# Where the operands of a split-float32 block kernel start in on-chip memory: multiples of 512 bytes

## The chip, the cores and the metric

One Trainium2 chip, one of its cores. The kernel is a hand-scheduled program for the five engines of that core: TensorE (PE, with its weight loads as PEld), VectorE (DVE), ScalarE (ACT), GpSimd (POOL) and SyncE (SP, used here to issue transfers). The metric is the device time of one execution in microseconds; times of the same kernel are medians of several runs.

## What is computed

The reference runs two transformer-like blocks over 256 tokens of 1024 features in float32.

```python
def reference(x, ...):
    x = first_block(x, ...)    # RMSNorm, gated delta rule (4 heads) and causal pooling, w_out;
                               # RMSNorm, product-key experts: 16,384 experts, 8 heads, top 16 of 128 x 128 keys;
                               # RMSNorm
    return second_block(x, ...)  # RMSNorm, block attention (8 heads) and retention (4 heads), w_out;
                                 # RMSNorm, FFN of 2816 with a depthwise convolution and GELU;
                                 # per-layer embedding with a sigmoid gate; RMSNorm
```

The experts in the reference are gathered per token; their core is

```python
u = expert_down[idx]
v = expert_up[idx]
act = jax.nn.gelu(jnp.einsum("td,thkd->thk", xb, u).astype(jnp.float32), approximate=False)
return jnp.einsum("thk,thkd->td", (gate * act).astype(v.dtype), v)
```

## The kernel before, in words

**Weights as a stream of tiles.** All weights are laid out as 412 tiles of 128 x 1024 float32, in the order of use: 20 tiles of the first projection, 8 of the first output projection, 16 of the query, 128 of `expert_down`, 128 of `expert_up`, then the second block (8 + 8 + 12 tiles of its input projections, 8 of its output projection, 1 of the embedding, 22 triples of up, gate and down, 1 of the embedding, 8 of its gate). The experts are not gathered: every expert is computed for every token, and a dense table of gates, zero but for the chosen ones, multiplies the result.

**Splitting.** A float32 product is made of three products of the type `fp32r`. SP loads a tile into one of four slots of `raw` (L335). ACT rounds it into `whi` (L443), and DVE subtracts, giving `wlo` (L456); each has four slots. The activations are split in the same way into `ahi` and `alo`, each expert's row of `ea` into `phi` (ACT, L1289) and `plo` (DVE, L1854), and the embedding's operand into `pthi` and `ptlo` once. The helper `products` (L459 to L462) issues the three matmuls:

```python
nc.tensor.matmul(out_ap, wh, xh, start=first, stop=False, skip_group_check=True)
nc.tensor.matmul(out_ap, wh, xl, start=False, stop=False, skip_group_check=True)
return nc.tensor.matmul(out_ap, wl, xh, start=False, stop=last, skip_group_check=True)
```

The second argument is the stationary operand, the third the moving one. There are two uses. `gemm_tile` makes 24 products per weight tile: stationary 128 columns of `whi` or `wlo`, moving 256 columns of `ahi` or `alo`. `token_rows` makes 12 per weight tile: stationary 128 tokens of an activation, moving 512 columns of `whi` or `wlo`. The activation is `ahi`/`alo` in the output projections, the values and the embedding's gate, `phi`/`plo` in the 128 tiles of `expert_up` and the 22 down tiles of the FFN, and `pthi`/`ptlo` in the 2 embedding tiles (these call `products` at L1018). A small product at the start has the 8 columns of `gw_hi` or `gw_lo` stationary and `ahi` or `alo` moving. All other products are plain float32.

**Addresses.** `place` gives every buffer the same start in each of the 128 partitions. It rounds sizes up to 32 bytes and puts the next buffer behind. The first free byte is 16,481, rounded up to 16,512. By these sizes `raw`, `whi`, `wlo`, `ahi`, `alo`, `ident` and `ones` all start 128 bytes past a multiple of 512, as does every 128-column slice of them. `vec` (772 bytes, rounded to 800), `warm` and `wm` (32 each) come next, so `xt`, `pf`, `phi`, `plo` and the arena `ea` start 480 past a multiple of 512. The arena is reused by the stages; there `pthi` and `ptlo` start 96 past, `AmT2` 32 past, `gbc` 448 past, and the slices of `gw_hi` and `gw_lo`, 32 bytes each, at various multiples of 32.

**Order of the work.** Each engine has its own program, in order; semaphores join them. ACT may refill `whi` slot j once PE has finished the tile four before (`w_used`); SP refills `raw` once both halves of the split are made. A 16-way scatter per head puts the gates into the dense table in DRAM: POOL issues 256 indirect transfers (L409), 128 for each half of the tokens. POOL does some of the second half's between heads of the first, the rest after. SP fetches gates for four experts at a time into `gd` (L343); for tiles 0 to 87 of `expert_up` those of the first half of the tokens, since the rows of the second half need the second chain of scatters. Ahead of the pair of fetches of tile 88 SP waits for that chain:

```python
with sp.Fori(1, SPLIT // 8) as j:
    up_pair(j, P)
sp.wait_ge(s["scat1"], 16 * TOPK * NH)
with sp.Fori(SPLIT // 8, N_EXP // 8) as j:
    up_pair(j, T)
```

`up_pair` issues both the fetches of gates and the loads of the weight tiles, so a wait there holds back the weights as well. DVE multiplies `ea` by `gd` (L1850), ACT makes `phi`, DVE `plo`, PE the 12 products.

`ones` is filled by DVE at the start (L1496). PE uses it for idle products at the start (L577) and for sums over partitions in the first block's mixer (L631, L740). ACT reads one element of it in six short activations (L1118 and others) that have the engine's tables loaded ahead of time.

Of the kernel before, what the change touches and what calls it, by code (L numbers as in the profile page):

```python
# [20 lines left out]
ACT = mybir.ActivationFunctionType  # L21
AX = mybir.AxisListType

P = 128
# [3 lines left out]
KT = D // P  # L28
# [54 lines left out]
N_CV = _c  # L83
# [16 lines left out]
def program(nc, x_tok, vecs, wts, c1, gate_w, rows, w_pool, keys, c2, ple_t, nrows, out):  # L100
    ctx = ExitStack()
    with ctx:
        s = {n: ctx.enter_context(nc.semaphore("s_" + n)) for n in SEMS}


        top = [-(-nc.sbuf_base // 32) * 32]
        slab = ctx.enter_context(nc.sbuf_tensor("slab", [P, (nc.sbuf_bytes_remaining - 64) // 4], F32))

        def place(name, shape, dt=F32, at=None):
            size = int(np.prod(shape)) * (2 if dt == F16 else 4)  # L110
            size = -(-size // 32) * 32
            if at is None:
                at, top[0] = top[0], top[0] + size
            else:
                at[0], at = at[0] + size, at[0]
            return nc.alloc_sbuf_tensor_at(name, [P] + list(shape), dt, offset=at)

        raw = place("raw", [2, 2 * TW])
        whi = place("whi", [RING, TW], F32R)
        wlo = place("wlo", [RING, TW], F32R)  # L120
        ahi = place("ahi", [KT, T], F32R)
        alo = place("alo", [KT, T], F32R)
        ident = place("ident", [P])
        ones = place("ones", [P])
        vec = place("vec", [N_CV])
        warm = place("warm", [8])
        wm = place("wm", [KT])
        eps = warm[:, 6:7]
        small = top[0]
        xt = place("xt", [TB, D])  # L130
        pf = place("pf", [2, T])
# [35 lines left out]
        arena = top[0]  # L167
        ea = place("ea", [N_EXP, T])
        end = top[0]
        assert end <= nc.sbuf_usable_end, end  # L170

        a = [arena]
        h32 = place("h32", [KT, T], at=a)
# [50 lines left out]
        gw_lo = place("gw_lo", [KT, 8], F32R, at=a)  # L224
        ba = place("ba", [T], at=a)
        tok = place("tok", [160], at=a)
        assert a[0] <= end, a[0] - end
        col = {}
        c = 0
# [7 lines left out]
        a = [common]  # L237
# [4 lines left out]
        a = [arena + 4 * T * sc_at]  # L242
# [3 lines left out]
        a = [common]  # L246
# [57 lines left out]
        def half_row(buf, b0):  # L304

            return buf[:, b0 // 2, (b0 % 2) * 512:(b0 % 2 + 1) * 512]
# [799 lines left out]
        def _(act):  # L1106
            A = nc.scalar.activation

            def row_squares(i, c, src, junk):

                A(junk, src, ACT.Square, accum_out=ss[:, i, c:c + 1]).then_inc(s["t_sq"], 1)
# [3 lines left out]
                A(root[:, i, tb:tb + 1], ss[:, i, c:c + 1], ACT.Sqrt, scale=1.0 / D, bias=bias).then_inc(s["t_root"], 1)  # L1115

            act.wait_ge(s["ones_ready"], 1)
            A(warm[:, 0:1], ones[:, 0:1], ACT.Sqrt)  # L1118
            act.wait_ge(s["x_in"], 16)
            row_squares(0, 0, xt[:, 0, :], sq_t[:, 0, :])  # L1120
            act.wait_ge(s["t_sq"], 1)
# [15 lines left out]
            def hi_for(u):  # L1137

                split_hi(act, u + LEAD, (u + LEAD) % 4)
# [62 lines left out]
            def pool_rows(p):  # L1202

                act.wait_ge(s["pool_ps"], p + 1)
                for g in (2 * p, 2 * p + 1):
                    m = A(h32[:, DH + g, :], bank(0, T, base=g * T), ACT.Copy, scale=vcol("pool_scale", g))
                m.then_inc(s["mix_pool"], 1)
                act.wait_ge(s["mix_pool"], p + 1)
                operand_act(act, 1, h32, QUARTERS[p])

            pool_rows(0)
            A(warm[:, 7:8], ones[:, 0:1], ACT.Sqrt)
            for p in range(2):
                act.wait_ge(s["o_ps"], 2 * p + 2)
                A(sq[:, 2 * p:2 * p + 2, :], bank(6 + p, 2 * T).rearrange("p (h t) -> p h t", h=2), ACT.Square)\
# [117 lines left out]
                turned_act(act, 3, q, mid_weight)  # L1333
            hi_for(W_V2 - 1)
            hi_for(W_V2)
            A(warm[:, 2:3], ones[:, 0:1], ACT.Sqrt)
            for tb in range(TB):
                act.wait_ge(s["xd"], 3 + tb)
                row_squares(2, tb, xt[:, tb, :], sq_t[:, tb, :])
# [111 lines left out]
            for q in range(2, 4):  # L1451
                turned_act(act, 6, q, ple_weight)
            hi_for(W_PLEG)
            A(warm[:, 3:4], ones[:, 0:1], ACT.Sqrt)
            for tb in range(TB):
                act.wait_ge((s["xa"], s["xd"])[tb], (2, 6)[tb])
                row_squares(6, tb, xt[:, tb, :], sq_t[:, tb, :])
# [1 line left out]
            A(root[:, 6, :], ss[:, 6, 0:TB], ACT.Sqrt, scale=1.0 / D, bias=eps).then_inc(s["t_root"], 1)  # L1459
            for n in range(1, KT):  # L1460
                hi_for(W_PLEG + n)
            A(warm[:, 4:5], ones[:, 0:1], ACT.Sigmoid)
            act.wait_ge(s["t_r"], 9)
            for b0 in range(3):
                act.wait_ge(s["gate_ps"], b0 + 1)
# [4 lines left out]
            for c in range(2):  # L1470
# [3 lines left out]
                if c == 0:  # L1474
                    act.wait_ge(s["x5"], 3)
                    row_squares(7, 2, half_row(xt, 2), half_row(sq_t, 2))
            A(warm[:, 5:6], ones[:, 0:1], ACT.Sqrt)  # L1477
            act.wait_ge(s["t_sq"], 16)
            act.wait_ge(s["t_pre"], 4)
            row_root(7, 0, 1, pre[:, 3, 0:1])  # L1480
# [708 lines left out]
```

## Time and profile before

| | us |
|---|---|
| median of 3 runs | 1329.18 |
| lowest, highest | 1328.83, 1330.32 |
| profiled execution: span from first to last instruction | 1327.4 |
| TensorE matmul busy | 1310.4 |
| VectorE busy | 943.1 |
| ScalarE busy | 725.3 |
| GpSimd busy | 517.7 |

The median counts the whole execution, the span only what lies between the first and the last instruction of one profiled execution; this one's own time outside the span is not given beside it. Busy time of TensorE is the union of its matmuls, whose ends are modelled: a duration of one matmul is longer than the distance to the next one's start. The granted clock of TensorE is written in tenths of full speed. Line numbers (L456) are those of the kernel before.

### The profile page before, as it was taken

The numbers are of one execution on the slowest core, as the hardware profiler recorded it, in microseconds if no ns is written. First come the engines' busy times: TensorE is split into PE (matmuls) and PEld (weight loads), VectorE is DVE, ScalarE is ACT, GpSimd is POOL, SyncE is SP. The second block draws the span as 40 slices with busy tenths as digits, with TensorE's granted clock in tenths as the row PEclk, the third lists the DMA queues.
The fourth block names the chain that finished last, engine by engine and source line by source line (L and its number), as shares of the span: only waits on it lengthen the run. The fifth ranks groups of instructions, "written<-read, shape, count | busy, mean of one in ns | idle before, by whom it ended". The sixth has DMA issues, their size and how long they took to land. (4 is left out here: it accounts for less than half of the span.)

```text
span 1327.4 us, 26387 instructions
## 1 busy us (share of the span) xinstructions
PE 1310.4 (99%) x8853; PEld 1196.9 (90%) x8853; DVE 943.1 (71%) x1766; ACT 725.3 (55%) x1077; POOL 517.7 (39%) x276
## 2 busy tenths in 40 slices
PE   8999999999999999999999999999999999999997
PEld 8999899999999999998888888788789888999986
DVE  6885677999998467766666666666666667676665
ACT  6833557777777743344444444444465446444446
POOL 1010002888887888787787778100000000000000
PEclk9999999999999999999999999999999999999999
DMA  7459554777767766668777778777674335555551
GB/s 257 149 194 383 197 175 154 180 185 184 183 177 186 191 168 153 142 146 216 209 208 211 213 213 209 262 234 228 213 242 162 112 115 183 181 188 183 184 191 64
DMA packets 119325, 253.03 MB, mean 191 GB/s; under 512 B 44336, under 2 KB 60848, under 8 KB 118752
## 3 DMA queue, kind: packets, MB, share of 16 engines
q1 hardware_dynamic: 77232, 229.24, 53.5%
q0 software_dynamic: 42032, 22.99, 10.9%
q8 instruction: 36, 0.59, 0.2%
q14 instruction: 25, 0.20, 0.0%
HBM read 234.23 MB, written 17.96 MB: 190 GB/s over the span
## 5 line engine op out<-in xcount | busy, mean ns | idle before, releaser
L456 DVE TENSOR_TENSOR wlo<-raw,whi 128x1024 fp32r<-128x1024 f32 x412 | 503.1, 1223 | 156.3 <-ACT whi L443 147.5
L443 ACT ACTIVATE whi<-raw 128x1024 fp32r<-128x1024 f32 x412 | 435.1, 1058 | 305.8 <-PE ps L462 292.8
L409 POOL DMA_INDIRECT gates_dense<-gate,spot x256 | 506.1, 1977 | 170.2 <-issue 78.7
L460 PE MATMUL ps<-ahi,whi 128*128 128x256 f32 x1824 | 522.5, 286 | 2.9 <-DVE alo L537 2.6
L461 PE MATMUL ps<-alo,whi 128*128 128x256 f32 x1824 | 515.9, 283 | 0.0
L462 PE MATMUL ps<-ahi,wlo 128*128 128x256 f32 x1824 | 515.7, 283 | 0.0
L460 PEld LDWEIGHTS ps<-ahi,whi 128*128 128x128 f32 x1824 | 349.9, 192 | 7.5 <-issue 5.8
L461 PEld LDWEIGHTS ps<-alo,whi 128*128 128x128 f32 x1824 | 349.4, 192 | 0.9
L462 PEld LDWEIGHTS ps<-ahi,wlo 128*128 128x128 f32 x1824 | 349.4, 192 | 0.0
L460 PE MATMUL ps<-whi,phi 128*128 128x512 f32 x600 | 238.2, 397 | 1.2 <-DVE plo L1854 1.1
L462 PE MATMUL ps<-whi,plo 128*128 128x512 f32 x600 | 237.8, 396 | 0.0
L461 PE MATMUL ps<-wlo,phi 128*128 128x512 f32 x600 | 237.7, 396 | 0.0
L1854 DVE TENSOR_TENSOR plo<-ea,phi 128x256 fp32r<-128x256 f32 x128 | 54.5, 426 | 126.9 <-ACT phi L1289 120.2
L460 PEld LDWEIGHTS ps<-whi,phi 128*128 128x128 f32 x600 | 113.0, 188 | 28.8 <-issue 1.1
L462 PEld LDWEIGHTS ps<-whi,plo 128*128 128x128 f32 x600 | 113.0, 188 | 27.5
L461 PEld LDWEIGHTS ps<-wlo,phi 128*128 128x128 f32 x600 | 113.1, 188 | 26.5
L1278 ACT ACTIVATE ea<-ps 128x256 f32 x120 | 46.1, 384 | 134.5 <-PE ps L462 134.3
L460 PE MATMUL ps<-whi,ahi 128*128 128x512 f32 (+1 forms) x136 | 52.4, 385 | 0.1
L461 PE MATMUL ps<-wlo,ahi 128*128 128x512 f32 (+1 forms) x136 | 51.3, 377 | 0.0
L462 PE MATMUL ps<-whi,alo 128*128 128x512 f32 (+1 forms) x136 | 51.3, 377 | 0.0
L427 POOL DMA_DIRECT2D wrow<-in_nrows x1 | 0.6, 580 | 126.6 <-DVE plo L1854 126.6
L1289 ACT ACTIVATE phi<-ea 128x256 fp32r x120 | 47.9, 399 | 0.0
(367 smaller groups left out, 1088.0 us busy)
## 6 DMA issues: line engine op xcount, KB each, us to landing
raw<-in_wts SPq DMA_DIRECT2D x412, 512.0 KB, 3.7
gates_dense<-pf POOLq DMA_DIRECT2D x4, 4096.0 KB, 30.8
gd<-gates_dense SPq DMA_DIRECT2D x22, 256.0 KB, 4.8
gd<-gates_dense SPq DMA_DIRECT2D x10, 512.0 KB, 5.8
gates_dense<-gate,spot POOLq DMA_INDIRECT x256
cst<-in_c POOLq DMA_DIRECT2D x1, 1216.0 KB, 6.5
xt<-in_x_tok SPq DMA_DIRECT2D x2, 512.0 KB, 4.5
kk<-in_keys POOLq DMA_DIRECT2D x1, 1024.0 KB, 5.2
```

The lines of the kernel that those rows point to most:

```text
L409: pl.indirect_dma_start(out=dense, out_offset=bass.IndirectOffsetOnAxis(ap=spot[:, tb, h, k:k + 1], axis=0), in_=gate[:, tb, h, k:k + 1], ...
L427: pl.dma_start(wrow[:, :, :].rearrange("p a n -> p (a n)"), nrows.partition_broadcast(P)).then_inc(s["nrows_in"], 16)
L443: nc.scalar.activation(whi[:, j, :], raw_tile(j // 2, j % 2), ACT.Copy).then_inc(s["w_hi"], 1)
L456: nc.vector.tensor_tensor(wlo[:, j, :], raw_tile(j // 2, j % 2), whi[:, j, :].bitcast(F32), ALU.subtract).then_inc(s["w_lo"], 1)
L460: nc.tensor.matmul(out_ap, wh, xh, start=first, stop=False, skip_group_check=True)
L461: nc.tensor.matmul(out_ap, wh, xl, start=False, stop=False, skip_group_check=True)
L462: return nc.tensor.matmul(out_ap, wl, xh, start=False, stop=last, skip_group_check=True)
L1278: A(row_of(quad * 4 + n), late(n if four else n % 2, T), ACT.Gelu).then_inc(s["gelu"], 1)
L1289: A(phi[:, n % 2, :], row_of(quad * 4 + n), ACT.Copy).then_inc(s["p_hi"], 1)
L1854: V.tensor_tensor(plo[:, n % 2, :], row_of(oct_ * 8 + n), phi[:, n % 2, :].bitcast(F32), ALU.subtract)\
```

## The change

`place` rounds the start of every buffer of 1024 bytes or more up to a multiple of 512, in the main area and in the arena. The small buffers `vec`, `warm` and `wm` move ahead of the weight buffers, so that nothing small lies between the large ones; `ident`, 512 bytes, keeps its place behind `alo`. With the same first free byte, `raw` then starts at 17,408 where it started at 16,512, and `raw`, `whi`, `wlo`, `ahi`, `alo` and `ident` all move by 896 bytes; `xt`, `pf`, `phi`, `plo` and the arena start at multiples of 512 too, as do `pthi` and `ptlo` in it. `ones` moves into the arena of the first stage, behind `tok`. The six short activations of ACT read `eps`, which lies in `warm`, in place of an element of `ones`. No instruction is added or removed, and no wait.

```diff
+        LINE = 512
...
         def place(name, shape, dt=F32, at=None):
             size = int(np.prod(shape)) * (2 if dt == F16 else 4)
             size = -(-size // 32) * 32
-            if at is None:
-                at, top[0] = top[0], top[0] + size
-            else:
-                at[0], at = at[0] + size, at[0]
+            at = top if at is None else at
+            if size >= 1024:
+                at[0] = -(-at[0] // LINE) * LINE
+            at[0], at = at[0] + size, at[0]
             return nc.alloc_sbuf_tensor_at(name, [P] + list(shape), dt, offset=at)
 
+        vec = place("vec", [N_CV])
+        warm = place("warm", [8])
+        wm = place("wm", [KT])
+        eps = warm[:, 6:7]
         raw = place("raw", [2, 2 * TW])
...
         ident = place("ident", [P])
-        ones = place("ones", [P])
-        vec = place("vec", [N_CV])
-        warm = place("warm", [8])
-        wm = place("wm", [KT])
-        eps = warm[:, 6:7]
         small = top[0]
...
         tok = place("tok", [160], at=a)
+        a[0] = -(-a[0] // LINE) * LINE
+        ones = place("ones", [P], at=a)
...
-            A(warm[:, 0:1], ones[:, 0:1], ACT.Sqrt)
+            A(warm[:, 0:1], eps, ACT.Sqrt)
...
```

The last pair of lines stands for six of its kind.

## Rows read from the trace of the kernel before

**Rows 1.** The page: the span, the matmuls' busy share, the granted clock in 40 slices.
```profile
span 1327.4 us, 26387 instructions
PE 1310.4 (99%) x8853; PEld 1196.9 (90%) x8853; DVE 943.1 (71%) x1766; ACT 725.3 (55%) x1077; POOL 517.7 (39%) x276
PEclk9999999999999999999999999999999999999999
```

**Rows 2.** PE's waits: who was waited for, total us, times, longest us.
```profile
PE ps L460 <- DVE plo L1854: 1.1, 2, 0.7
```

**Rows 3.** Timeline of PE, hidden stage: start us, duration us, `ahi` against `whi`.
```profile
300.20 0.28 PE L460 MATMUL ps<-ahi,whi 128*128 128x256 f32 x1
...
302.36 0.28 PE L460 MATMUL ps<-ahi,whi 128*128 128x256 f32 x1
```

**Rows 4.** Line 460 alone: min/median/max ns, first and last start.
```profile
L460 PE MATMUL ps<-ahi,whi x1824: 277/283/387, 11.5 to 1285.2; 128*128 128x256 f32 x183
...
L460 PE MATMUL ps<-whi,phi x600: 392/397/500, 604.7 to 1290.8; 128*128 128x512 f32 x150
```

**Rows 5.** Timeline of PE, values of the second block: stationary `ahi`/`alo`.
```profile
976.94 0.39 PE L461 MATMUL ps<-wlo,ahi 128*128 128x512 f32 x1
...
978.98 0.39 PE L461 MATMUL ps<-wlo,ahi 128*128 128x512 f32 x1
```

**Rows 6.** Timeline of PE, output stage of the experts: stationary `phi`/`plo`.
```profile
700.42 0.39 PE L460 MATMUL ps<-whi,phi 128*128 128x512 f32 x1
...
702.06 0.39 PE L461 MATMUL ps<-wlo,phi 128*128 128x512 f32 x1
```

**Rows 7.** Timeline of PE, second embedding tile: stationary `pthi`/`ptlo`.
```profile
1291.48 0.40 PE L460 MATMUL ps<-whi,pthi 128*128 128x512 f32 x1
...
1292.65 0.39 PE L462 MATMUL ps<-whi,ptlo 128*128 128x512 f32 x1
```

**Rows 8.** Timeline of PE, 8 stationary columns of `gw_hi` and `gw_lo`.
```profile
17.99 0.28 PE L461 MATMUL ps<-alo,gw_hi 128*8 128x256 f32 x1
...
18.67 0.28 PE L461 MATMUL ps<-alo,gw_hi 128*8 128x256 f32 x1
```

**Rows 9.** Plain float32 products by form: busy us, mean ns, idle us before.
```profile
L681 PE MATMUL ps<-Dm,AmT 128*128 128x128 f32 x48 | 6.5, 281 | 0.2
L681 PE MATMUL ps<-Dm,gbc 128*128 128x128 f32 x48 | 6.4, 279 | 0.2
```

**Rows 10.** Timeline of ACT, the first of the six short activations.
```profile
2.05 0.20 ACT L1118 ACTIVATE warm<-ones 128x1 f32<-128x1 f32 x1
```

**Rows 11.** The SP queue's waits: its wait for the second chain of scatters.
```profile
SPq L365 <- DMA gates_dense<-gate,spot: 3.9, 1, 3.9
```

**Rows 12.** Timeline of PE around the start of tile 86 of `expert_up`.
```profile
846.38 0.40 PE L462 MATMUL ps<-whi,plo 128*128 128x512 f32 x1
846.63 0.50 PE L460 MATMUL ps<-whi,phi 128*128 128x512 f32 x1
846.97 0.39 PE L461 MATMUL ps<-wlo,phi 128*128 128x512 f32 x1
```

**Rows 13.** Timeline of POOL, scatters from 618 us to the last.
```profile
620.96 2.50 POOL L409 DMA_INDIRECT gates_dense<-gate,spot  x1 [0.30 <-issue]
...
629.39 1.54 POOL L409 DMA_INDIRECT gates_dense<-gate,spot  x1 [0.30 <-issue]
631.24 1.54 POOL L409 DMA_INDIRECT gates_dense<-gate,spot  x1 [0.30 <-issue]
...
657.84 2.18 POOL L409 DMA_INDIRECT gates_dense<-gate,spot  x1 [4.40 <-DMA gates_dense<-gate,spot]
...
829.01 2.50 POOL L409 DMA_INDIRECT gates_dense<-gate,spot  x1 [0.30 <-issue]
831.82 2.51 POOL L409 DMA_INDIRECT gates_dense<-gate,spot  x1 [0.30 <-issue]
833.76 1.18 POOL L425 DMA_DIRECT2D h<-in_x_tok  x1
```

More of the change, by code:

```diff
@@ L170, in program @@
         assert end <= nc.sbuf_usable_end, end
+        assert arena % LINE == 0
         a = [arena]
@@ L1211, in _ @@
             pool_rows(0)
-            A(warm[:, 7:8], ones[:, 0:1], ACT.Sqrt)
+            A(warm[:, 7:8], eps, ACT.Sqrt)
             for p in range(2):
@@ L1335, in _ @@
             hi_for(W_V2)
-            A(warm[:, 2:3], ones[:, 0:1], ACT.Sqrt)
+            A(warm[:, 2:3], eps, ACT.Sqrt)
             for tb in range(TB):
@@ L1453, in _ @@
             hi_for(W_PLEG)
-            A(warm[:, 3:4], ones[:, 0:1], ACT.Sqrt)
+            A(warm[:, 3:4], eps, ACT.Sqrt)
             for tb in range(TB):
@@ L1461, in _ @@
                 hi_for(W_PLEG + n)
-            A(warm[:, 4:5], ones[:, 0:1], ACT.Sigmoid)
+            A(warm[:, 4:5], eps, ACT.Sigmoid)
             act.wait_ge(s["t_r"], 9)
@@ L1476, in _ @@
                     row_squares(7, 2, half_row(xt, 2), half_row(sq_t, 2))
-            A(warm[:, 5:6], ones[:, 0:1], ACT.Sqrt)
+            A(warm[:, 5:6], eps, ACT.Sqrt)
             act.wait_ge(s["t_sq"], 16)
```

## The prediction

> **What bounds the kernel now.** I read the page's busy lines first: TensorE's matmuls fill 99% of the span and every other engine is well below [rows 1]. Then PE's waits: the row shown, 1.1 us, is one of six, and all six come to 7.1 us in 1327.4 [rows 2]. The granted clock is at its upper level, 2.4 GHz, in all but the last of the 40 slices [rows 1]. So no engine and no transfer has to be earlier; only a change in the pitch of the matmuls themselves (start of one to start of the next), or a new wait ahead of PE, can move the end.
>
> The duration of a matmul in the listing holds its pipeline and is longer than its pitch, so pitches come from start times.
> - 256 columns, `ahi` against `whi`: 18 products in 2.16 us, 120.0 ns each [rows 3]. The group holds 3 x 1824 of them [rows 4].
> - 512 columns of `whi`, stationary `ahi`: 9 products in 2.04 us, 226.7 ns each [rows 5].
> - 512 columns of the same `whi`, stationary `phi`: 7 products in 1.64 us, 234.3 ns each [rows 6]. The group holds 3 x 600 [rows 4]. Twelve such products are one tile: 2.81 us.
> - stationary `pthi`, another stage: 5 products in 1.17 us, 234.0 ns each [rows 7]. There are 3 x 8.
> - 256 columns of `ahi` against the 8 columns of `gw`: 6 in 0.68 us, 113.3 ns each [rows 8].
>
> At 2.4 GHz 512 columns last 213.3 ns and 256 last 106.7 ns. The overhead is therefore 13.3 ns in both of the first two forms, whatever the width, 21 ns with `phi` or `pthi`, and 6.6 ns with eight weight columns. It goes with the stationary tile. What sets `phi` and `pthi` apart from `ahi` is the address: `phi` lies at 480 and `pthi` at 96 after a multiple of 512, which is 32 past a multiple of 64 for both; `ahi`, `alo`, `whi` and `wlo` lie at 128, a multiple of 64. Width, data type, moving buffer and clock are the same, and `phi` and `pthi` are in different stages with different neighbours. I take the address as the cause.
>
> **The change part by part.**
> *`phi`, `plo`, `pthi`, `ptlo` to multiples of 512.* The trace has no product with operands there. Bounds: nothing gained (234.3), and the 220.0 ns that results if the 6.7 ns between `whi` and `gw` went too (226.7 - 6.7). I take 226.7, the nearest row: same width, same moving buffer, a stationary tile of the same size at a multiple of 64. Per product 7.6 ns, per tile of twelve 91 ns. Such tiles: 128 in the output stage of the experts, 22 in the FFN, 2 for the embedding, 152: 152 x 0.091 = 13.9 us if PE is never held up.
>
> *`raw`, `whi`, `wlo`, `ahi`, `alo` from 128 to 0.* All move by the same 896 bytes, so the distances between them stay. Taken at nothing, since no row shows what 128 costs against 0; the bound on the side of a gain is the `gw` pitch, 6.7 ns a product (a rival below); on the side of a loss nothing is excluded, the `phi` overhead of 21 ns being the nearest price for a worse address, but 0 is a multiple of all that 128 is. The fp32 products give no help: `AmT2` (AmT in the row) lies at 32, `gbc` at 448, and they differ by 2 ns in duration where `phi` and `ahi` differ by 7 [rows 9]; these take the array twice as long per column, so they may have slack to hide it.
>
> *Vector and scalar operands, DMA destinations.* ACT and DVE are 55% and 71% busy, DMA moves 191 GB/s in the mean, and PE waits 7.1 us for all of them: no gain can come of them except through the chain below. *`ones`, `vec`, `warm`, `eps` moved, six table warm-ups read `eps`:* the same number of instructions, one element read as before (0.2 us, [rows 10]), `eps` set before `ones` on DVE and under the same semaphore. Nothing; if all six cost 0.1 us more, two on the tail would show, 0.2 us.
>
> **Where part of the gain is late next.** The second scatter chain on the POOL queue must be complete before SP fetches the gates of tile 88. SP waits 3.9 us for it now [rows 11], its weight loads queued behind. These come late, and at 846.63, the start of tile 86 (the first `phi` product starts at 604.7 [rows 4]; 241.9 / 2.81 = 86), PE stands 0.1 us: 846.38 to 846.63 is 0.25 and the next piece is 0.34, where 0.23 is usual [rows 12]. So the slack is used up, and every further microsecond by which PE comes earlier than the scatters is lost once. PE would come 86 x 0.091 = 7.8 us earlier. The scatters: of the 81 intervals between starts from 606 to 832, 50 are 2.81 us, the pitch of PE's tiles and so of DVE's and ACT's work on them; 20 are 1.85 to 1.93; the others are mixed or are waits for a landing [rows 13]. The 50 that keep step with the tile shorten with it: 50 x 0.091 = 4.6 us. The rest stays. (The Trainium skill, SBUF — State Buffer, in the section Who interferes with whom, says that a DVE instruction with two SBUF inputs and a GpSimd instruction that reads SBUF exclude one another, the later one waiting. By that rule a scatter is released when the DVE's subtract ends, once a tile, and the 4.6 us are right; the pitch in the rows agrees, though no row names the release.)
> Bounds: the chain keeps its end (0 us), or keeps up wholly (7.8). I take 4.6. PE waits 3.2 us at tile 86.
>
> Sum: 4.6 up to tile 86, then 42 tiles of the experts and 22 of the FFN and 2 of the embedding, 66 x 0.091 = 6.0. Together 10.6 us. With the bounds of the chain: 6.0 and 13.8. The profiled execution has a span of 1327.4 us; the median is 1329.18, 1.8 above, for what lies outside the span and for the run. I subtract from the median: **1318.6**; bounds 1315.4 and 1323.2.
>
> **The rivals.**
> *A, the above,* 0.64.
> *B, 512 matters for every operand.* All products fall to the level of `gw`: 113.3 and 220.0 ns. For: an overhead of 13.3 ns that does not depend on the width is what one extra piece at an unaligned start would give, and whatever starts at 128 with 512 bytes straddles a multiple of 512, as no `gw` slice does. Against: eight columns are simply fewer to load. Time: 36 tiles of 24 and 8 of 12 products ahead of the scatters, 6.4 us, which start the chain earlier; 50 x 0.172 = 8.6 in the chain (172 ns = 12 x 14.3; the 128 tiles of the hidden stage gain 20.6 but then wait for the chain); 66 x 0.172 = 11.4 after; 64 tiles of 24 products later, 10.3; 24 tiles of 12, 1.9. Together 38.6: 1290.6. Chance 0.12.
> *C, the address has no part in it.* `phi` is slower for another reason (it is rewritten each tile while PE reads its neighbour), and nothing changes: 1329.2. This is the case too where the change does not do what it says. Against: `pthi` is written once, long before the second pair of its products is read, and shows the same 234 [rows 7]. Chance 0.16. (The Trainium skill, SBUF — State Buffer, Specifications, gives lines of 16 bytes. By that alone every address here, a multiple of 32, is aligned already, and the time is that of C. The 7.6 ns between rows 5 and 6 speak against it.)
> *D, the scatters fall worse.* The one way to the other side that I can price: at a tile pitch of 2.72 the 20 short intervals also lock to the tile, each 0.87 us longer, 17.4 in all; the chain ends 17.4 - 4.6 = 12.8 later, PE stands until then at tile 86, and 6.0 come back after: 1329.2 + 6.8 = 1336.0. It decides once 13 of the 20 lock ((4.6 + 6.0) / 0.87). Against: the short ones stand in the same place of each head's round. Chance 0.08.
>
> **How the numbers follow.** A measurement of this kernel tells 0.2%, 2.7 us, from no change. A's whole range is faster by more, as is B: 0.76 faster. C is the same: 0.16. D is slower: 0.08. The range takes in A and C, and goes down to 1308, where over a third of B's extra 28 us is added; it leaves out B in full and D, 0.20. A's own range is 1315 to 1323.5.
>
> **What would show each step.** A: starts of the `phi` products 226 to 228 ns apart, tiles of 2.72 us, the `ahi`/`whi` products still at 120; scatters in the output stage mostly 2.72 apart, SP's wait for them about 7 us and PE's wait near tile 86 about 3 us. B: 256-column products at 113. C: 234 still. D: the last scatter after 840 us. The forecast is wrong if the `phi` pitch stays, if the 120 ns moves, or if the scatters end elsewhere than 829 us.

## The result, and the profile after

The changed kernel takes 1333.06 us in the median of 11 runs (1330.19 to 1334.26), the kernel before 1329.23 (11 runs): a ratio of 1.0026, with a 95% interval of 1.0019 to 1.0034. It is slower, by a quarter of a percent, where I forecast 0.8% faster. The first step of the forecast came true, and the rival that I gave 0.08 took more than all of it back.

The page of the changed kernel: span, busy time, granted clock (line numbers are 3 higher than before). It answers to [rows 1].

```profile
span 1331.4 us, 26387 instructions
PE 1300.3 (98%) x8853; PEld 1197.8 (90%) x8853; DVE 942.2 (71%) x1766; ACT 725.5 (54%) x1077; POOL 525.0 (39%) x276
PE   8999999999999999999999999599999999999997
PEclk9999999999999999999999999799999999999999
```

TensorE is busy for 10.1 us less, and the span is 4.0 us longer. There is a hole in slice 26, and the clock dips in the same slice. First the pitch of the `phi` products, in the timeline of PE (start us, duration us), to be held against [rows 6]:

```profile
700.12 0.39 PE L463 MATMUL ps<-whi,phi 128*128 128x512 f32 x1
...
701.71 0.39 PE L464 MATMUL ps<-wlo,phi 128*128 128x512 f32 x1
```

Seven products in 1.59 us, 227 ns each, where 234.3 were. A tile takes 2.72 us. The `ahi`/`whi` products stay at 120. Then the hole. PE's waits [rows 2], longest in total first, and in the second fence the SP queue's wait for the scatters [rows 11]:

```profile
PE ps L463 <- DVE plo L1857: 14.9, 3, 14.0
PE ps L463 <- DVE alo L540: 2.8, 4, 1.3
```

```profile
SPq L368 <- DMA gates_dense<-gate,spot: 16.7, 1, 16.7
```

SP waits 16.7 us for the second chain of scatters where it waited 3.9, and PE stands at tile 86, as named, but for 14 us and not for 3. The timeline of PE there answers to [rows 12]. Each line of the windows behind it gives the stretch and its length, busy time and count of PE, PEld, DVE, ACT and POOL, the granted clock, the DMA share and GB/s:

```profile
838.62 0.39 PE L465 MATMUL ps<-whi,plo 128*128 128x512 f32 x1
853.02 0.80 PE L463 MATMUL ps<-whi,phi 128*128 128x512 f32 x1 [14.02 <-DVE plo L1857]
853.61 0.63 PE L464 MATMUL ps<-wlo,phi 128*128 128x512 f32 x1
...
857.45 0.58 PE L464 MATMUL ps<-wlo,phi 128*128 128x512 f32 x1
857.87 0.39 PE L465 MATMUL ps<-whi,plo 128*128 128x512 f32 x1
```

```profile
853.00:858.00 5.00, 4.98 (x12) 3.97 (x13) 3.24 (x5) 0.76 (x2) 0.00 (x0) 0.52 0.90 293
858.00:868.00 10.00, 10.00 (x46) 8.24 (x45) 5.79 (x10) 5.46 (x8) 0.00 (x0) 1.00 0.50 151
```

After the wait the granted clock is 0.52 in the mean of 5 us, almost all of it at the lower level, 1.2 GHz; products whose starts were 227 ns apart now start 427 ns apart. The 11 products from 853.02 to 857.87 take 4.85 us where 2.49 would do: 2.4 us on top of the wait. The last scatters, against the last of [rows 13]:

```profile
835.56 2.42 POOL L412 DMA_INDIRECT gates_dense<-gate,spot  x1 [0.30 <-issue]
838.28 1.54 POOL L412 DMA_INDIRECT gates_dense<-gate,spot  x1 [0.30 <-issue]
840.13 1.54 POOL L412 DMA_INDIRECT gates_dense<-gate,spot  x1 [0.31 <-issue]
```

The last one starts at 840.1 and not at 831.8. So the sum of the changed kernel: the output stage starts at 604.7 us before and 604.8 now. Tile 86 starts 6.4 us later (853.0 for 846.6). That is less than the 8.3 of the last scatter: SP issued the fetch of gates that waits for the chain 6.0 us after the last scatter's start (837.8) and now issues it 3.3 us after it (843.4); why, no run here shows. The low clock costs 2.4 more, and the shorter pitch gives back 4.8 until the end of the span, 4.0 later.

**Why the scatters became slower.** Of the 81 intervals between scatters from 606 us on, 20 were under 2.0 us before and 8 are now. The kernel before, DVE from 626.46 and POOL at 626.58 (the next scatter, at 629.39 and of 1.54 us, stands in [rows 13]):

```profile
626.46 1.22 DVE L456 TENSOR_TENSOR wlo<-raw,whi 128x1024 fp32r<-128x1024 f32 x1
627.59 0.29 DVE L1850 TENSOR_TENSOR ea<-ea,gd 128x128 f32 x1
629.05 0.43 DVE L1854 TENSOR_TENSOR plo<-ea,phi 128x256 fp32r<-128x256 f32 x1 [1.17 <-ACT phi L1289]
629.39 1.26 DVE L456 TENSOR_TENSOR wlo<-raw,whi 128x1024 fp32r<-128x1024 f32 x1
```

```profile
626.58 2.51 POOL L409 DMA_INDIRECT gates_dense<-gate,spot  x1 [0.30 <-issue]
```

The scatter of 626.58 starts 0.12 us after the subtraction `wlo` and ends at 629.09, 1.41 us after `wlo` does (627.68); free, a scatter takes 1.54. It reads as if it were held until the subtraction ends. The multiplication behind it does not matter: in the hidden stage nothing follows `wlo`, and the distance between the two ends is the same. There, in the kernel before, DVE and POOL:

```profile
453.78 1.23 DVE L456 TENSOR_TENSOR wlo<-raw,whi 128x1024 fp32r<-128x1024 f32 x1 [1.65 <-ACT whi L443]
```

```profile
454.09 2.34 POOL L409 DMA_INDIRECT gates_dense<-gate,spot  x1 [0.30 <-issue]
```

The ends are 455.01 and 456.43, 1.42 us apart. Of 139 scatters in this trace that start inside a subtraction, 137 end 1.41 to 1.43 us after its end, 63 of them with a multiplication behind it and 10 with nothing.

The next scatter can start 0.30 us later, at 629.39, 1.71 us after the subtraction's end; the next `wlo` normally starts 1.59 after it. But once in eight tiles DVE's loop turns, and everything is 0.12 us late (idle 1.17 where it is 1.05): here `wlo` starts at 629.39 too, and the scatter is not held. The one after it finds DVE idle. In the changed kernel, at the same kind of place:

```profile
647.67 1.22 DVE L459 TENSOR_TENSOR wlo<-raw,whi 128x1024 fp32r<-128x1024 f32 x1
648.80 0.28 DVE L1853 TENSOR_TENSOR ea<-ea,gd 128x128 f32 x1
650.16 0.43 DVE L1857 TENSOR_TENSOR plo<-ea,phi 128x256 fp32r<-128x256 f32 x1 [1.08 <-ACT phi L1292]
650.50 1.22 DVE L459 TENSOR_TENSOR wlo<-raw,whi 128x1024 fp32r<-128x1024 f32 x1
```

```profile
647.88 2.42 POOL L412 DMA_INDIRECT gates_dense<-gate,spot  x1 [0.30 <-issue]
650.61 2.53 POOL L412 DMA_INDIRECT gates_dense<-gate,spot  x1 [0.30 <-issue]
```

The tile is 0.09 us shorter, so `wlo` starts 0.09 earlier in respect of the scatter: at the turn of the loop the scatter comes 0.11 too late and is held as all the others are. Before, the escape had had next to no margin: it needed a shift of less than 0.1 us to go. (The Trainium skill, SBUF — State Buffer, section Who interferes with whom, states the exclusion of a DVE instruction with two SBUF inputs and a GpSimd one that reads SBUF; the trace agrees, with 2.51 for 1.54 us and the end of the hold at the end of the one instruction.)

### The profile page after: what moved, and what is told of

Same layout as the page of the kernel before. It is cut to its first block and busy times, and to the rows that moved or that the text cites. A ratio compares the mean times of both kernels' runs of the same rounds, so it can differ in the third digit from the quotient of the medians.

```text
span 1331.4 us, 26387 instructions
## 1 busy us (share of the span) xinstructions
PE 1300.3 (98%) x8853; PEld 1197.8 (90%) x8853; DVE 942.2 (71%) x1766; ACT 725.5 (54%) x1077; POOL 525.0 (39%) x276
## 5 line engine op out<-in xcount | busy, mean ns | idle before, releaser
L412 POOL DMA_INDIRECT gates_dense<-gate,spot x256 | 513.5, 2006 | 170.1 <-issue 79.0
L463 PE MATMUL ps<-whi,phi 128*128 128x512 f32 x600 | 235.2, 392 | 15.0 <-DVE plo L1857 14.9
L464 PE MATMUL ps<-wlo,phi 128*128 128x512 f32 x600 | 234.6, 391 | 0.0
L465 PE MATMUL ps<-whi,plo 128*128 128x512 f32 x600 | 234.2, 390 | 0.0
L463 PEld LDWEIGHTS ps<-whi,phi 128*128 128x128 f32 x600 | 113.3, 189 | 39.5 <-DVE plo L1857 14.8
L464 PEld LDWEIGHTS ps<-wlo,phi 128*128 128x128 f32 x600 | 113.3, 189 | 22.8
```

The source lines that it names most:

```text
L412: pl.indirect_dma_start(out=dense, out_offset=bass.IndirectOffsetOnAxis(ap=spot[:, tb, h, k:k + 1], axis=0), in_=gate[:, tb, h, k:k + 1], ...
```

## The experiments

All of them are edits of the changed kernel. A time with a ratio is a median of several executions, set against the kernel before, with a 95% interval; a time without one is a single execution. The letters A to D are the prediction's cases.

**Multiples of 64 in place of 512.**

```diff
-        LINE = 512
+        LINE = 64
...
+        top[0] = -(-top[0] // 512) * 512 + 64
         raw = place("raw", [2, 2 * TW])
```

> Everything of 1024 bytes or more at a multiple of 64, the main area 64 past a multiple of 512. Theory (64 is what counts): the phi products stay 226.7 ns apart, ahi/whi products 120.0, the time is that of the changed kernel, 1333, with the same long wait at the scatters. Rival (512 is what counts): the phi products are 230 ns apart or more, and as PE is held less by the scatters the time falls towards 1329.

1332.29 us, ratio 1.0024 (1.0015 to 1.0034); `phi` products 226.7 ns apart, `ahi`/`whi` 120, last scatter at 838.4. The same as the change, for these products and for the time. The 512 has no part in it.

**`phi`, `plo` and `ea` back.** `PAST` are buffers that `place` does not round; `h32`, `sq` and `sc` share `ea`'s place.

```diff
+        PAST = ('phi', 'plo', 'ea', 'sc', 'h32', 'sq')
...
-            if size >= 1024:
+            if name in PAST:
+                at[0] += 32 if name == 'phi' else 0
+            elif size >= 1024:
```

> The changed kernel with phi, plo and the arena's ea back to 32 past a multiple of 64, all else where the change put it. Theory (the pitch of these products alone changed everything, the scatters lost their short intervals through it): phi products 234.3 ns apart, pthi products 226.7, last scatter starts near 832, SP waits about 4 us for the chain, PE stands 0.1 us there, time 1329.0. Rival (the scatters are slower because their own operands gate and spot, or those of DVE, lie elsewhere): pitch 234.3, but the last scatter still near 840, PE stands 6 us, time 1336.

1327.54 us, ratio 0.9988 (0.9979 to 0.9998). The timeline of PE, and SP's wait:

```profile
700.21 0.40 PE L468 MATMUL ps<-wlo,phi 128*128 128x512 f32 x1
...
701.84 0.40 PE L469 MATMUL ps<-whi,plo 128*128 128x512 f32 x1
```

```profile
SPq L372 <- DMA gates_dense<-gate,spot: 4.5, 1, 4.5
```

Seven products in 1.63 us: 233 ns, a nanosecond less than before; over the 1800 `phi` products that is the 1.7 us by which this kernel is faster than the kernel before. The last scatter starts at 830.9, 19 intervals are under 2.0 us, and PE does not stand. With (nearly) the old pitch the scatters are as they were, though their operands `gate` and `spot` and those of DVE's subtraction lie where the change put them. So the pitch did it; a tile of 2.80 us still leaves the escape, one of 2.72 does not.

**The other operands off by 32.** In the first, `PAST = ('whi', 'wlo')` with 32 added at `whi`; in the second, `('ahi', 'alo')` with 32 at `ahi`; `LINE` is 64 in both.

> whi and wlo 32 past a multiple of 64, the rest at multiples of 64. Theory (only the stationary operand's start counts): ahi/whi products of 256 columns, where whi is stationary, 127.6 ns apart in place of 120.0; phi products, where whi moves, stay at 226.7. 5472 x 7.6 ns = 41.6 us more, of which 14 to 16 come back because PE no longer waits for the scatters: about 1357 to 1361. Rival (either operand's start counts): phi and ahi products of 512 columns also 7.6 ns longer, 2184 x 7.6 = 16.6 us on top, about 1375.

> ahi, alo and ident 32 past a multiple of 64, the rest at multiples of 64. Theory (only the stationary operand's start counts): ahi/whi products of 256 columns, where ahi moves, stay at 120.0; the 360 products of 512 columns with ahi or alo stationary go from 226.7 to 234.3, 2.7 us: 1336. Rival (the moving operand counts too): the 256-column products are 127.6 apart, about 1360.

1314.14 and 1314.94 us: both faster than either kernel, which no theory of mine allowed. The timeline of PE with `ahi` off, hidden stage and output stage:

```profile
300.00 0.28 PE L468 MATMUL ps<-ahi,whi 128*128 128x256 f32 x1
...
302.10 0.28 PE L468 MATMUL ps<-ahi,whi 128*128 128x256 f32 x1
...
700.37 0.39 PE L468 MATMUL ps<-whi,phi 128*128 128x512 f32 x1
...
701.77 0.39 PE L468 MATMUL ps<-whi,phi 128*128 128x512 f32 x1
```

18 products in 2.10 us, 116.7 ns: three less than the 120.0 of both kernels. Six in 1.40, 233.3 ns. And here `phi` lies at a multiple of 64 and so does `whi`, but the one at 64 and the other at 0 past a multiple of 512. In the kernel with `whi` off, where `phi` lies 32 past `whi`, the numbers are the same. My cause, a stationary tile off a multiple of 64, has fallen. What fits all the kernels so far is the distance between the two operands of a product: 0 gives 120.0 for 256 columns and 226.7 for 512; 32 gives 116.7 for 256; 32 and 64 give 233.3 for 512. In the kernel before `phi` was 352 off, modulo 512, and at 234.3. A distance helps products of 256 columns and hurts those of 512. (Here the scatters held nobody: tiles of 2.80 us leave the escape, 24 intervals of 79 under 2.0 us with `whi` off.)

**Setting the distances.** `raw`, `whi`, `wlo` and `phi` at 128 past a multiple of 512, `ahi` and `alo` `APART` further.

```diff
-        LINE = 512
+        LINE, FIRST, APART = 512, 128, 32
+        lined = lambda x: -(-(x - FIRST) // LINE) * LINE + FIRST
...
-            if size >= 1024:
-                at[0] = -(-at[0] // LINE) * LINE
+            if name in ('ahi', 'alo'):
+                at[0] += APART if name == 'ahi' else 0
+            elif size >= 1024:
+                at[0] = lined(at[0])
```

(`vec`, `warm` and `wm` go back behind `ident`.) With `APART` 32, 64 and 128:

> raw, whi, wlo, phi, plo, pthi, ptlo all 128 past a multiple of 512, ahi and alo 160 past. Theory (what counts is whether the stationary and the moving operand start at the same place modulo 64 or 128: equal gives 120.0 for 256 columns and 226.7 for 512, unequal 116.7 and 233.3): ahi/whi products 116.7, phi products 226.7, ahi products of 512 columns 233.3. Without a wait for the scatters 1329.2 - 18.1 - 13.7 + 2.4 = 1299.8; they hold PE by 10 to 17 us: 1310 to 1317. Rival (one tile off 64 anywhere puts all products into the second pair of values, as the phi products of the last run did): phi at 233.3 and 1314.

> As the run with 32, but ahi and alo 64 further than whi and wlo (192 past a multiple of 512). If equality modulo 64 is what counts: ahi/whi 120.0, all products of 512 columns 226.7, about 1333. If modulo 128 or more: ahi/whi 116.7, phi 226.7, ahi of 512 columns 233.3, 1310 to 1317.

> Distance 128 for ahi and alo, no reductions. If only the distance modulo 128 counts: ahi/whi 120.0, all products of 512 columns 226.7, 1333. If modulo more than that: 113 to 118 and 1319 to 1325 as with 64, the scatters holding PE some 20 us.

| `APART` | `ahi`/`whi`, 256 columns | `phi`, 512 | `ahi`, 512 | PE stands at tile 86 | us |
|---|---|---|---|---|---|
| 0 (all at multiples of 64) | 120.0 | 226.7 | 227 | 12 | 1332.29, ratio 1.0024 (1.0015 to 1.0034) |
| 32 | 116.7 | 226.7 | 233 | 19 | 1323.85, ratio 0.9957 (0.9942 to 0.9972) |
| 64 | 113.3 and 116.7 to 117.8 | 226.7 | 233 | 23 | 1323.24 |
| 128 | 118.4 to 119.9 | 226.7 | 231 to 233 | 16 | 1332.13 |

With 32, the timeline of PE:

```profile
300.07 0.28 PE L467 MATMUL ps<-ahi,whi 128*128 128x256 f32 x1
...
302.17 0.28 PE L467 MATMUL ps<-ahi,whi 128*128 128x256 f32 x1
...
700.13 0.39 PE L467 MATMUL ps<-whi,phi 128*128 128x512 f32 x1
...
701.49 0.39 PE L467 MATMUL ps<-whi,phi 128*128 128x512 f32 x1
```

Both kinds now have their better value, and each kind follows its own distance within one kernel. The rival of that run is out, and so is equality modulo 64 or 128 alone, as 64 and 128 both act. The time lay above my 1310 to 1317, since the scatters held PE longer than I allowed: PE is at tile 86 earlier still, at 828.4, and the last scatter starts at 835.5. With 128 neither of my two lines came out: the values lie between those of 0 and of 32, and as the scatters hold PE in any case, the little that is gained does not reach the end. The five `pthi` products of [rows 7], which these edits moved without aiming at it, also show values in between: 226.8 ns at a distance of 0 (changed kernel), 229.6 at 192 (multiples of 64), 231.6 at 256 (`ahi` off), 233.8 at 224 (`whi` off).

**Scatters left out.** The 16 of the last head of the second half of the tokens, and 16 x 16 less in SP's wait.

```diff
-            for q in range(ahead, NH * TOPK):
+            for q in range(ahead, (NH - 1) * TOPK):
```

> The changed kernel without the 16 scatters of the last head for the second half of the tokens (their gates stay zero). Theory (the wait for the scatters and the clock that falls in it are all that hides the gain): the chain ends 40 us earlier, SP does not wait, PE does not stand, the clock does not fall, and the time is 1329.2 - 13.8 = 1315.4. Rival (something else has become longer by some us): above 1318.

1316.46 us. SP does not wait for the scatters, and PE's waits begin:

```profile
PE ps L463 <- DVE alo L540: 2.8, 4, 1.3
PE ps L565 <- ACT h L1129: 1.4, 1, 1.4
```

16.6 us less than the changed kernel, against 14.0 of wait and 2.4 of low clock. As far as one execution can tell, nothing else was hiding the gain.

**The escape given back.** `idle` is a spare buffer; `delay` is `(0,)` in tiles 0 to 87, empty after.

```diff
+                if n in delay:
+                    V.tensor_reduce(idle[:, :], vec[:, 0:150].unsqueeze(1).to_broadcast([P, 2, 150]), AX.X, ALU.max)
                 u = W_UP + n + LEAD
                 if not last or n < 7:
                     split_lo(dve, None, u % 4, oct_ * 2 + u // 4)
```

> The changed kernel, with one DVE reduction of 300 elements ahead of the weight split in one tile of eight, in tiles 0 to 87 of the output stage (about 0.3 us each, in DVE's idle time). Theory (a scatter that starts after DVE's run of two-input operations has begun waits until its end, and the shorter tile took away the only moments at which it started before): a short interval returns after each of these, 8 to 16 more than the 7 of the changed kernel, the last scatter starts at 815 to 832, PE stands 0 to 8 us there, time 1315 to 1324. Rival (the scatters are slow for another reason): last scatter near 840, 1333.

1317.62 us, ratio 0.9915 (0.9897 to 0.9933). More work on DVE makes the changed kernel faster by 15 us. 21 intervals are under 2.0 us, the last scatter starts at 824.6, and PE's waits for `plo` are back at [rows 2]:

```profile
PE ps L464 <- DVE plo L1858: 1.1, 2, 0.7
```

The mechanism of the scatters is thus shown by putting it back at the changed kernel's own pitch. The reduction takes 0.46 us and not 0.3.

**Both together.** `APART` of 32 or 64 and `delay` of `(2, 6)` or `(0, 2, 4, 6)`.

> The kernel with ahi and alo 32 bytes off whi, wlo and phi, and with the DVE reduction in two tiles of eight. Theory (the two effects are separate and add): ahi/whi 116.7, phi 226.7; about 22 short intervals return where there were 7, each worth 1.2 to 1.5 us, the last scatter starts at 803 to 812 in place of 835.5, PE stands 0 to 4 us there and the clock does not fall: 1301 to 1305. Rival (the chain is already as short as the output stage allows, 1.4 us per reduction no longer holds): last scatter after 820, time above 1308.

> The same with a distance of 64. Without the reductions its ahi/whi products were 113.3 ns apart for part of the hidden stage and 116.7 to 117.8 elsewhere. If that holds: 1298 to 1304, PE standing up to 6 us as it comes earlier; if the 113.3 does not return in another execution, as with the distance of 32.

> As the first, with the reduction in four tiles of eight. Theory: the last scatter starts before 805 and PE does not stand at all, 1299 to 1303. Rival (reductions too close cost DVE or find the scatter still running): no better than two of eight.

32 and two reductions in eight tiles: 1302.93 us (1302.76 to 1303.1), ratio 0.9802 (0.9786 to 0.9819). The last scatter starts at 799.3, earlier than I wrote: 43 intervals are under 2.0 us. The page, and in the second fence the reduction's line with min/median/max ns, first and last start:

```profile
span 1300.9 us, 26409 instructions
PE 1283.8 (99%) x8853; PEld 1180.1 (91%) x8853; DVE 951.2 (73%) x1788; ACT 726.0 (56%) x1077; POOL 490.1 (38%) x276
PEclk9999999999999999999999999999999999999999
```

```profile
L1872 DVE TENSOR_REDUCE idle<-vec x22: 457/459/459, 601.4 to 830.2; 128x2 f32<-128x300 f32 x22
```

Four reductions in eight tiles: the last scatter at 787.6, and 1302.64 us, ratio 0.9799 (0.9783 to 0.9816), the same; once PE does not stand, an earlier chain is worth nothing. A distance of 64: 1306.29, ratio 0.9805 (0.977 to 0.984), with one execution of four at 1297.31; the profiled one, 1306.71, has `ahi`/`whi` at 117 to 118 ns, in the hidden stage too. The 9 us between the executions are about what the 3072 products of the hidden stage would give at 114.4 ns, their mean in the run without reductions (an estimate, 3072 x 3.1 ns: the execution of 1297.31 us has no trace). So 64 has at least two paces, and which one an execution takes stays open.

## Why the prediction was wrong

The step that failed is the chain of scatters: it was to end 4.6 us earlier and ended 8.3 us later. Step by step:

- *Pitch of the `phi` products, 226.7.* Right in size, and wrong in cause. I named the stationary operand's start modulo 64. The run with `ahi` off has `phi` at a multiple of 64 and 233.3; what the runs follow is the distance between the two operands. The change set it to 0 for `phi`, as it was for `ahi` and `whi` before, and so my nearest row gave the right number by luck. Only [rows 8] could have warned me: the slices of `gw` lie at even and odd multiples of 32 by turns, and all are at 113.3.
- *`raw`, `whi`, `wlo`, `ahi`, `alo`: nothing.* Right: they moved together, and 120.0 stayed.
- *Other operands, `ones`, `eps`: nothing.* Right to about 1 us, by the run without 16 scatters.
- *152 tiles by 91 ns, 13.9 us.* Without the wait it was 12.8 (1329.2 - 1316.5). Most of the rest is the FFN, where a tile of 12 goes from 2.80 to 2.75 us and not from 2.81 to 2.72, 0.8 us over 22 tiles: the first products behind those of 256 columns have a longer pitch. In the trace of the changed kernel:

```profile
1170.58 0.40 PE L463 MATMUL ps<-whi,phi 128*128 128x512 f32 x1
...
1171.97 0.39 PE L463 MATMUL ps<-whi,phi 128*128 128x512 f32 x1
...
1173.33 0.28 PE L463 MATMUL ps<-ahi,whi 128*128 128x256 f32 x1
```

  Six in 1.39 us, 231.7 ns, then six in 1.36. Over the 20 FFN tiles that the trace has whole the means are 231.2 and 226.7; in the kernel before they were 233.6 and 233.3.
- *The chain: 50 x 0.091 = 4.6 us earlier, "The rest stays".* This step failed, and the sign of the whole with it. That a held scatter is let go when the subtraction ends was right, and the intervals that keep step did shorten to 2.72. But of the 20 short ones 12 went, at 0.87 us each, 10.4 us; and the six intervals that hold a wait for a landing came to 37.9 us for 35.3, 2.6 more, for which no run shows the cause. Less the 4.6, that is the 8.3 us by which the chain ended later. I had counted the short ones and had not asked why they were short. The answer was in the trace of before: DVE's idle of 1.17 us at the turn of the loop, and a scatter and `wlo` both starting at 629.39, with next to no margin against a shorter tile.
- *PE waits 3.2 us at tile 86.* It waited 14. Place and path were right. The clock that falls in such a wait, 2.4 us, was in no term; nothing before had shown a wait that long after the start.
- *Case D.* Its mechanism is what happened; that its time came near, 1336.0 for 1333.1, is partly luck. Not 20 short intervals locked but 12, and by D's own sum (12 x 0.87 - 4.6 - 6.0) that leaves the time where it was. The measured 3.9 us come of terms that it did not have: 2.6 for the landings and 2.4 for the low clock; 4.8 and not 6.0 came back after tile 86; and tile 86 followed the last scatter 1.9 us sooner. What I wrote against it, that the short ones stand in the same place of each round, spoke for it: what recurs at one place hangs on the phase of two loops, and the change moved one of them. 0.08 was too little for a mechanism that needed a shift of less than 0.1 us.
- *Case C.* Out: with nothing but addresses changed, 234.3 became 226.7.
- *Case B* rested on the 113.3 ns of `gw`. In the changed kernel no slice of `whi` or `gw` crosses a multiple of 512, and `ahi`/`whi` stays at 120 while `gw` goes up to 117; with all at multiples of 64 it is back at 113.7. With `APART` 64 it goes from 117 to 113.3 within its 24 products, though nothing moves. What sets it stays open.
- *A reading.* I wrote that the clock is at its upper level in all but the last slice; [rows 1] shows a 9 in all 40. No term rests on it.

## What to carry to other kernels

Where a chain on another engine already uses up its slack, a faster bound engine gains nothing until the chain is looked at by itself: ask of each of its durations, the short ones above all, what lets it be short, and whether that survives the new pitch. Where a few free moments decide, as here for the scatters that GpSimd starts between DVE's subtractions, a small operation in DVE's idle time can be worth more than its cost. Place the two operands of a split-float32 product by their distance, and measure both distances for each width: here 0 for 512 columns, 32 for 256.

## What the runs showed of the hardware

- The pitch of `fp32r` products depends on the distance between stationary and moving operand in a partition: 120.0 ns against 116.7 for 256 columns, 226.7 against 233.3 for 512, with opposite signs. At 128 the values lie between: 118.4 to 119.9 and 231 to 233. A distance of 64 can give 113.3 ns for 256 columns, in some stages and executions only. Why, no run here tells.
- At distance 0 the better value is not there at once: the first six 512-column products behind 256-column ones in the FFN average 231.2 ns in the changed kernel, the next six 226.7.
- After 14.0 us without a matmul the clock was at 1.2 GHz for 11 products, which cost 2.4 us; after 19.0 us, in the kernel with distance 32, for only six, which cost 1.4 us.
- A scatter that starts inside a DVE subtraction of two SBUF operands ends 1.41 to 1.43 us after the subtraction's end (137 of 139 in the kernel before), up to 2.5 us after its own start in place of 1.54, and the next start, 0.30 us later, keeps it in step with DVE's loop.
